# A two-layer hybrid trunk on one core: the mask product of the SSD rows left out, and new orders of work at four places

## The chip, the cores and the metric

The kernel runs on one core of a Trainium2 chip. The metric is the device time of one execution in microseconds. Of the kernel before there are three runs, 1043.61 to 1047.78, median 1046.85.

## The reference

One inference step of a decoder trunk with two layers, for 256 prompt tokens and 8 samples of 4 tokens, 288 columns that share all weights. The model width is 1024.

- Layer 0: norm, one input projection, then two head groups side by side: mLSTM (4 heads, key 128, value 256, with a gated state matrix) and SSD (16 heads of 64 in two groups that share B and C). Their outputs are joined for one output projection and added to the residual. A gated FFN with a causal convolution follows.
- Layer 1: norm, projection, retention (8 heads with rotary positions, value 256), output projection, residual and the same FFN. A last norm ends it.

What the change touches most is the SSD. For a head with running sums `acum` of its log decays it computes

```
seg   = acum[l] - acum[s]
decay = where(causal, exp(where(causal, seg, 0)), 0)
M     = (C B^T) * decay * dt
y     = M x + (C S) * exp(acum)
```

The log decays are negative, so `seg` is at most 0 wherever the mask holds. The states of all heads are outputs too.

## The kernel before, in words

**Weights and tiles.** Every matrix product has fp32 accuracy from three passes of fp32r: a weight chunk (128 x 1024, 512 KB, eight 128 x 128 blocks) is loaded to `raw`, ScalarE copies it to the high part `wh` (`split`, line 1222), VectorE subtracts to the low part `wl` (`split`, line 1627), and TensorE makes high x high, high x low and low x high (lines 806 to 808). All three buffers are rings of four chunks: SyncE's `stream` loads chunk c once the low part of chunk c-4 is made, ScalarE overwrites a slot once TensorE has read the chunk there. An output tile is 128 x 288 and takes eight blocks of K (24 matmuls), or more. The two mixer output projections have K = 16 blocks; their tiles go in groups of four, first halves first, so of the 16 chunks of the even one (numbered 0 to 15 here, from `E_OUT`) 0 to 3 are the first halves of tiles 0 to 3, 4 to 7 their second halves, 8 to 11 the first halves of tiles 4 to 7.

**Order.** Each engine has one program, an order written out by hand; semaphores join them. TensorE weaves head work between tiles. Its small products ("jobs", named `ass2.3`, `sbc5` and so on) and tiles use eight PSUM banks. `plan_banks` (lines 134 to 289) walks through TensorE's order and gives each job the next bank of a ring: "five" is banks 3 to 7, "mix" banks 4 to 7; tiles of the projections to the inside have banks 0 to 2, other tiles 0 to 3. Before a product TensorE waits until the former user of its bank is emptied (`claim`), by VectorE ("dve") or ScalarE ("act") as the plan says.

**mLSTM heads** (four tiles to a head). TensorE's `updates_a` (line 922, matmul 927) makes eight state updates from `kgm` and `vst`, the values in three stacked parts: ScalarE copies two of them (line 1467), GpSimd subtracts for the third (line 2315), VectorE adds the result to the state (line 1901). GpSimd's loop (lines 2304 to 2318) keeps convolution rows (`keep_x`), makes the low parts of a finished head (`back`, line 2210), fills the next convolution rows, builds masked queries and then writes `vst`. ScalarE's loop starts on line 1446. VectorE adds the sample output to `num` (line 1895) before the updates.

**SSD passes** (eight, two heads each; lines 1066, 1507, 1988). For each head `log_rows` (line 868) makes a row matrix 128 x 416 in PSUM with two matmuls: identity x `drop`, the mask (0 or -1e30), and a broadcast of the row of running sums (`sbc`). ScalarE's `decays` (line 1478) does three exponentials with the key's negative sum as bias and writes `E2`, four slots. VectorE multiplies by the group's scores `cbm` (line 2001), TensorE makes the outputs (`sy`, line 1026). The scores come through `cb0` and `cb1`, which ScalarE copies out (`masked_scores`, line 1472). A pass also turns x (`xn`), multiplies a tile of the projections (`filler`), and late passes take in and update the sample states (`si`, `sx`, `su`); GpSimd scales those states (line 2347), `xt` and `xws` (lines 2013, 1519, 2344) prepare them.

**SyncE in the SSD stage** (lines 751 to 773). It loads 11 states, then for each of 16 updated states waits for VectorE's update, stores the state and loads a later one. For the first five it calls `stream` for one more chunk of the even projection ahead of that wait.

**Retention heads** (eight, lines 1183 to 1203 on TensorE, 2116 to 2147 on VectorE). In head h the results of head h-1 are normalised and turned back, VectorE's `back` (line 1740) applies gain and gate, ScalarE and GpSimd make high and low parts. The last head is woven into the first halves of the odd output projection; its tile 3 has bank 3.

## Time and profile before

| | |
|---|---|
| median of three runs | 1046.85 us |
| profiled execution, its own time | 1046.8 us |
| span of the profile | 1045.0 us |
| mean granted TensorE clock | 0.98 |
| TensorE busy | 993.7 us (95%) |
| VectorE, ScalarE, GpSimd busy | 751.0, 559.9, 382.0 us |
| matmuls of line 806 (high x high) into a `hH` tile | 1160, mean 305 ns |
| low parts, line 1627 | 257, mean 1255 ns |
| high parts, line 1222 | 257, mean 1057 ns |

Times are from the start of the span. Matmuls are pipelined, so the duration of one is longer than the distance from one start to the next. A number in square brackets behind a row of a timeline is the engine's idle time before it, with the instruction that ended it. The stages: mLSTM heads to about 198, SSD passes to 264, even projection to 343, FFN, odd layer from 555, its output projection from 765, FFN to the end.

### The profile page before, as it was taken

The numbers are of one execution on the slowest core, as the hardware profiler recorded it, in microseconds if no ns is written. First come the engines' busy times: TensorE is split into PE (matmuls) and PEld (weight loads), VectorE is DVE, ScalarE is ACT, GpSimd is POOL, SyncE is SP. The second block draws the span as 40 slices with busy tenths as digits, with TensorE's granted clock in tenths as the row PEclk, the third lists the DMA queues.
The fourth block names the chain that finished last, engine by engine and source line by source line (L and its number), as shares of the span: only waits on it lengthen the run. The fifth ranks groups of instructions, "written<-read, shape, count | busy, mean of one in ns | idle before, by whom it ended". The sixth has DMA issues, their size and how long they took to land.

```text
span 1045.0 us, 19169 instructions
## 1 busy us (share of the span) xinstructions
PE 993.7 (95%) x7256; PEld 943.6 (90%) x7256; DVE 751.0 (72%) x1326; ACT 559.9 (54%) x932; POOL 382.0 (37%) x599
## 2 busy tenths in 40 slices
PE   7999998898779999999999999999979999999996
PEld 6999887777579999999999999899979999999996
DVE  5767688777856899996547857767755599899442
ACT  6535666633535666665444356656645565565431
POOL 4003214134201677774004531232221277777100
PEclk9989999999999999999999999999989999999999
DMA  8463364452455545455444745775634555445541
GB/s 300 136 230 122 109 205 147 133 172 92 141 208 187 171 169 162 163 167 191 162 167 157 262 141 172 221 232 191 201 135 147 176 168 175 162 164 169 188 142 46
DMA packets 64685, 177.22 MB, mean 170 GB/s; under 512 B 5889, under 2 KB 24065, under 8 KB 64593
## 3 DMA queue, kind: packets, MB, share of 16 engines
q1 hardware_dynamic: 64304, 174.86, 50.3%
q8 instruction: 58, 0.95, 0.4%
q0 software_dynamic: 288, 1.12, 0.3%
q14 instruction: 35, 0.28, 0.1%
HBM read 154.92 MB, written 21.05 MB: 168 GB/s over the span
## 4 chain that ended last, share of the span: by engine, by line
PE 85%; DVE 6%; ACT 3%; issue 3%; DMA 2%; POOL 1%; SPq 0%; DVEq 0%; ACTq 0%; POOLq 0%
PE bank L806 25%; PE bank L808 25%; PE bank L807 24%; PE bank L852 2%; DMA raw<-wts 2%; ACT wh L1222 1%; DVE wl L1627 1%; PE bank L1162 1%; PE bank L1130 1%; PE bank L1092 1%; PE bank L864 1%; POOL sts L2347 1%; DVE E L2001 1%; PE bank L859 0%; PE bank L1136 0%
## 5 line engine op out<-in xcount | busy, mean ns | idle before, releaser
L1222 ACT ACTIVATE wh<-raw 128x1024 fp32r<-128x1024 f32 x257 | 270.6, 1057 | 329.5 <-PE bank L808 317.7
L1627 DVE TENSOR_TENSOR wl<-raw,wh 128x1024 fp32r<-128x1024 f32 x257 | 321.8, 1255 | 167.9 <-ACT wh L1222 165.9
L806 PE MATMUL bank<-hH,wh 128*128 128x288 f32 x1160 | 353.9, 305 | 6.4 <-DVE wl L1627 4.1
L807 PE MATMUL bank<-hL,wh 128*128 128x288 f32 x1160 | 346.8, 299 | 0.0
L808 PE MATMUL bank<-hH,wl 128*128 128x288 f32 x1160 | 345.9, 298 | 0.0
L806 PEld LDWEIGHTS bank<-hH,wh 128*128 128x128 f32 x1160 | 222.2, 192 | 10.0 <-DVE wl L1627 3.2
L807 PEld LDWEIGHTS bank<-hL,wh 128*128 128x128 f32 x1160 | 222.3, 192 | 0.5
L808 PEld LDWEIGHTS bank<-hH,wl 128*128 128x128 f32 x1160 | 222.6, 192 | 0.0
L1750 DVE SCALAR_TENSOR_TENSOR cy<-pad,vec,cy 128x304 f32<-128x304 f32 (+1 forms) x212 | 140.7, 664 | 4.6 <-ACT cy L1270 0.6
L2188 POOL COPY pad<-fst 128x16 f32<-128x16 f32 x88 | 94.4, 1077 | 67.3 <-DVE cy L1750 67.3
L806 PE MATMUL bank<-upH,wh 128*128 128x288 f32 x352 | 104.4, 297 | 0.0
L808 PE MATMUL bank<-HH,wl 128*128 128x288 f32 x352 | 104.4, 296 | 0.0
L806 PE MATMUL bank<-HH,wh 128*128 128x288 f32 x352 | 104.0, 296 | 0.0
L807 PE MATMUL bank<-upL,wh 128*128 128x288 f32 x352 | 103.8, 295 | 0.0
L808 PE MATMUL bank<-upH,wl 128*128 128x288 f32 x352 | 103.5, 294 | 0.0
L807 PE MATMUL bank<-HL,wh 128*128 128x288 f32 x352 | 102.6, 292 | 0.0
L2168 POOL TENSOR_TENSOR hF<-hF 128x288 f32<-128x288 f32 x35 | 30.0, 856 | 190.7 <-ACT hF L1241 181.1
L1270 ACT ACTIVATE cy<-pad,vec 128x304 f32<-128x304 f32 (+1 forms) x100 | 63.1, 631 | 13.0 <-DVE pad L1664 8.8
L807 PEld LDWEIGHTS bank<-HL,wh 128*128 128x128 f32 x352 | 67.1, 191 | 0.0
L808 PEld LDWEIGHTS bank<-upH,wl 128*128 128x128 f32 x352 | 66.3, 188 | 0.0
L806 PEld LDWEIGHTS bank<-HH,wh 128*128 128x128 f32 x352 | 66.1, 188 | 0.0
L807 PEld LDWEIGHTS bank<-upL,wh 128*128 128x128 f32 x352 | 66.1, 188 | 0.1
(336 smaller groups left out, 1611.8 us busy)
## 6 DMA issues: line engine op xcount, KB each, us to landing
raw<-wts SPq DMA_DIRECT2D x257, 512.0 KB, 3.3
st<-r_in SPq DMA_DIRECT2D x9, 512.0 KB, 6.5
r_out<-st SPq DMA_DIRECT2D x9, 512.0 KB, 4.4
st<-c_in SPq DMA_DIRECT2D x8, 514.0 KB, 6.9
c_out<-st SPq DMA_DIRECT2D x8, 514.0 KB, 5.2
sts<-h_in SPq DMA_DIRECT2D x12, 256.0 KB, 6.1
h_out<-sts SPq DMA_DIRECT2D x12, 256.0 KB, 2.9
st3r<-r_in SPq DMA_DIRECT2D x4, 512.0 KB, 6.1
```

Source lines behind the costliest of these rows:

```text
L806: mm(out, h, xh, start=(k == 0), stop=False)
L807: mm(out, h, xl, start=False, stop=False)
L808: last = mm(out, lo, xh, start=False, stop=(k == K - 1))
L852: last = nc.tensor.transpose(out[0:n, g * P:(g + 1) * P], src[:, a:a + n], ident)
L864: mm(out[:, 0:TP], k[:, 0:P], q[:, 0:TP], start=True, stop=True)
L1092: last = mm(out[:, 0:T], ones, xbcT[:, 4 * g + i, :], start=(i == 0), stop=(i == 3))
L1222: s.do(act(wh[:, c % RING, :], raw[:, c % RING, :], ACT.Copy), hi_ready)
L1270: s.do(act(cy[:, n % 4, 0:width], x[:, 0:width], ACT.Identity, scale=tap, bias=bias), tap_done)
L1627: do(tt(wl[:, c % RING, :], raw[:, c % RING, :], wh[:, c % RING, :].bitcast(F32), ALU.subtract), lo_ready)
L1750: do(stt(out=y, in0=x[:, j:j + width], scalar=taps[j], in1=y, op0=ALU.mult, op1=ALU.add), conv_done if j == len(taps) - 1 else None)
L2168: do(tt(hF[:, 0, :], hF[:, 0, :], hF[:, i, :], ALU.add), ssq_ready if i == KD - 1 else None)
L2188: do(copy(padded(x, w)[:, :, 0:w], kept), fill_done)
```

## The change

Five places change.
1. SSD rows: the mask product of `sbc` is left out. VectorE's gate code now keeps the positive sum as the key's column; ScalarE makes max(0, column - row) with a ReLU, three activations a head, waits for its own last one, then two exponentials a head of the negative, for two heads together. Where the mask does not hold this is 1, so the mask moves to the scores: VectorE writes `cbm` as (drop >= -1) x score. VectorE waits for the new semaphore `decay_ready`.
2. mLSTM heads: ScalarE's two copies to `vst` stand at the start of the head, GpSimd's `vst` part ahead of `keep_x`, and its `back` behind the fills and queries.
3. SyncE: chunks of the even projection are streamed to 7 before the first stored state, to 9 before the fourth, to 11 before the ninth (exclusive ends).
4. Last retention head on TensorE and in the plan: head 6 is turned back before head 7's sample output, and its late jobs use the ring "mix".
5. Last retention head on VectorE: `back` of head 6 first, statistics ahead of the early updates.

The diff, cut to its core:

```diff
@@ constants, planner of banks @@
+MASKED = ((slice(0, P), slice(0, TP + P)), (slice(0, NS), slice(TP + P, BLK)))
...
-    for name in ("cb0", "bn0", "bn1", "sbc0", "sbc1"):
+    job("cb0", "dve", "five")
+    for name in ("bn0", "bn1", "sbc0", "sbc1"):
         job(name, "act", "five")
...
         if i == 0:
-            job("cb1", "act", "five")
+            job("cb1", "dve", "five")
...
         tile(group_tile(h, 3))
-        job(f"ros{h}", "dve", "five")
+        ring = "mix" if h == CH - 1 else "five"
+        if h == CH - 1:
+            turned_back("r", h - 1, ring)
+        job(f"ros{h}", "dve", ring)
         for b in EARLY_STATES:
-            job(f"rss{h}.{b}", "dve", "five")
-        if h:
+            job(f"rss{h}.{b}", "dve", ring)
+        if 0 < h < CH - 1:
             turned_back("r", h - 1, "five")
@@ SyncE @@
             for n in range(BG * NB):
                 g, b = divmod(n, NB)
-                if n < 5:
-                    stream(E_OUT + 4 + n)
+                if n in (0, 3, NB):
+                    stream(E_OUT + {0: 7, 3: 9, NB: 11}[n])
@@ TensorE @@
-            def log_rows(name, part, h):
+            def log_rows(name, part, h, masked):
...
-                mm(out[:, 0:BLK], identR[:], drop[:], start=True, stop=False)
-                mm(out[:, 0:BLK], one, rowS[part], start=False, stop=True).then_inc(mix_done, 1)
+                if masked:
+                    mm(out[:, 0:BLK], identR[:], drop[:], start=True, stop=False)
+                mm(out[:, 0:BLK], one, rowS[part], start=not masked, stop=True).then_inc(mix_done, 1)
...
             def sbc(h):
-                log_rows(f"sbc{h}", PARTS["ac"], h)
+                log_rows(f"sbc{h}", PARTS["ac"], h, False)
...
                 group(h, 3)
+                if h == CH - 1:
+                    back("r", h - 1, AH + h - 1)
                 sample_out(h)
                 updates(h, EARLY_STATES)
-                if h:
+                if 0 < h < CH - 1:
                     back("r", h - 1, AH + h - 1)
@@ ScalarE @@
                 step_a(t)
+                wait_empty(eng, f"v{2 * h + 1}")
+                if h:
+                    wait_job(eng, f"ass{h - 1}.{NB - 1}")
+                for row in ROW[0:2]:
+                    s.do(act(vst[row, 0:AV + 1], values_a(h, 2)[0:NS], ACT.Copy), vst_hi)
...
                 product(f"asp{h}", pout[:, h % 2, 0:AV + 1])
-                if h:
-                    wait_job(eng, f"ass{h - 1}.{NB - 1}")
-                for row in ROW[0:2]:
-                    s.do(act(vst[row, 0:AV + 1], values_a(h, 2)[0:NS], ACT.Copy), vst_hi)
...
-            def masked_scores(g):
...
-            def decays(h):
+            def gaps(h):
...
-                c = P + h
-                s.do(act(x[:, 0:TP], b[:, 0:TP], ACT.Exp, bias=cols[:, 0, c:c + 1]))
-                s.do(act(x[:, TP:TP + P], b[:, TP:TP + P], ACT.Exp, bias=cols[:, 1, c:c + 1]))
-                s.do(act(x[0:NS, TP + P:BLK], b[0:NS, TP + P:BLK], ACT.Exp, bias=cols[0:NS, 2, c:c + 1]), mix_act)
+                for g, n, a, z in ((0, P, 0, TP), (1, P, TP, TP + P), (2, NS, TP + P, BLK)):
+                    s.do(act(x[0:n, a:z], b[0:n, a:z], ACT.Relu, scale=-1.0, bias=cols[0:n, g, P + h:P + h + 1]),
+                         mix_act if g == 2 else None)
+
+            def decays(i):
+                for h in (2 * i, 2 * i + 1):
+                    gaps(h)
+                s.settle()
+                for h in (2 * i, 2 * i + 1):
+                    for part in MASKED:
+                        s.do(act(E2[:, h % 4, :][part], E2[:, h % 4, :][part], ACT.Exp, scale=-1.0),
+                             decay_ready if part[0].stop == NS else None)
...
-            masked_scores(0)
...
             decays(0)
-            decays(1)
             inverse(AH - 1)
...
                     back("a", AH - 1, y_even)
-                    eng.wait_ge(st_out[2], 32)
-                    masked_scores(1)
@@ VectorE @@
-                do(ts(slab[b16, 1, :], ac[b16, :], -1.0, None, ALU.mult))
+                do(copy(slab[b16, 1, :], ac[b16, :]))
...
             normalise("a", AH - 1, AH - 1)
+            def masked_scores(g):
+                wait_job(eng, f"cb{g}")
+                b = mb(f"cb{g}")
+                for part in MASKED:
+                    do(stt(out=cbm[g][part], in0=drop[part].bitcast(F32), scalar=-1.0, in1=b[part],
+                           op0=ALU.is_ge, op1=ALU.mult), mix_dve if part[0].stop == NS else None)
+                settle()
+            masked_scores(0)
...
-                        wait_empty(eng, f"sbc{h}")
-                        if h == HG:
-                            wait_empty(eng, "cb1")
+                        eng.wait_ge(decay_ready, h + 1)
...
                 if i + 3 < PAIRS:
                     xn(i + 3)
+                if i == 0:
+                    eng.wait_ge(st_out[2], 32)
+                    masked_scores(1)
...
             split(R_OUT + 3 + 3)
+            back("r", CH - 2)
             sample_out(CH - 1)
+            statistics("r", CH - 1, AH + CH - 1)
             updates(CH - 1, EARLY_STATES)
-            statistics("r", CH - 1, AH + CH - 1)
-            back("r", CH - 2)
             normalise("r", CH - 1, AH + CH - 1)
@@ GpSimd @@
             for h in range(AH):
+                eng.wait_ge(vst_hi, 2 * h + 2)
+                settle()
+                do(tt(vst[ROW[2], 0:AV + 1], values_a(h, 2)[0:NS], vst[ROW[0], 0:AV + 1].bitcast(F32), ALU.subtract), vst_ready)
+                settle()
                 keep_x(3 + 2 * h)
                 keep_x(4 + 2 * h)
-                if h > 1:
-                    back("a", h - 2, y_even)
                 if h + 1 < AH:
                     fill_x(6 + 2 * h)
                     fill_x(7 + 2 * h)
                     queries("a", h + 1, h + 1, qT[:, h + 1, :])
...
+                if h > 1:
+                    back("a", h - 2, y_even)
                 if h + 1 < AH:
                     split_keys("a", h + 1, h + 1)
```

## Rows read from the trace of the kernel before

**Rows 1.** Table by stage: us, busy of PE PEld DVE ACT POOL, PEclk, DMA, GB/s
```profile
215.00:260.00 45.00, 41.10 (x289) 32.09 (x289) 32.32 (x56) 17.92 (x43) 16.17 (x12) 1.00 0.39 130
...
290.00:312.00 22.00, 16.01 (x106) 14.99 (x105) 10.87 (x20) 8.12 (x13) 1.97 (x2) 0.94 0.61 211
...
560.00:600.00 40.00, 40.00 (x302) 40.00 (x302) 34.64 (x54) 12.75 (x12) 25.15 (x14) 1.00 0.71 237
...
765.00:790.00 25.00, 19.51 (x138) 18.80 (x137) 15.20 (x35) 11.03 (x19) 3.93 (x6) 0.86 0.31 100
```

**Rows 2.** TensorE's list of waits: who for whom, us in total, times, longest
```profile
PE bank L806 <- DVE wl L1627: 9.4, 4, 5.3
...
PE bank L927 <- ACT kgs L1311: 3.2, 2, 1.6
```

**Rows 3.** Timeline of TensorE, state updates of heads 2 and 3: start, us, what, idle before
```profile
161.65 0.72 PE L927 MATMUL bank<-vst,kgm 96*128 96x258 f32 x4 [2.32 <-issue]
...
184.60 0.73 PE L927 MATMUL bank<-vst,kgm 96*128 96x258 f32 x4 [2.58 <-issue]
...
188.89 1.47 PE L927 MATMUL bank<-vst,kgm 96*128 96x258 f32 x4 [0.36 <-DVE num L1895]
```

**Rows 4.** Timelines of VectorE and ScalarE, last mLSTM head
```profile
175.01 1.23 DVE L1627 TENSOR_TENSOR wl<-raw,wh 128x1024 fp32r<-128x1024 f32 x1 [2.33 <-ACT wh L1222]
...
181.98 0.84 ACT L1467 ACTIVATE vst<-vA 32x257 fp32r<-32x257 f32 x2
```

**Rows 5.** Timeline of TensorE, log products of one SSD head
```profile
213.49 0.46 PE L872 MATMUL bank<-drop,identR 128*128 128x416 f32 x1
...
213.88 0.46 PE L873 MATMUL bank<-rowS,foldR 64*128 64x416 f32 x1
```

**Rows 6.** ScalarE's timeline (two rows), then groups of lines 1288 and 1687
```profile
199.44 0.45 ACT L1484 ACTIVATE E<-bank,cols 128x256 f32<-128x256 f32 x1
...
201.00 0.28 ACT L1316 ACTIVATE sm<-sm,vec 128x3 f32<-128x3 f32 x1
...
L1288 ACT ACTIVATE E<-cst x8: 533/552/554, 608.0 to 737.0; 128x416 f32<-128x416 f32 x8
...
L1687 DVE SCALAR_TENSOR_TENSOR Sp<-bank,E 128x384 f32<-128x384 f32 x4 | 2.2, 550 | 0.0
```

**Rows 7.** Timelines of VectorE and TensorE ahead of the SSD passes
```profile
201.55 0.16 DVE L1721 TENSOR_TENSOR sm<-sm 128x3 f32<-128x3 f32 x1 [3.02 <-ACT sm L1318]
...
204.51 1.15 PE L852 MATMUL bank<-cst,xbcT 128*128 128x128 f32 x9
```

**Rows 8.** Timelines of TensorE and VectorE, SSD passes
```profile
219.79 0.44 PE L1032 MATMUL bank<-E,xdt 128*64 128x256 f32 x2 [1.03 <-DVE E L2001]
...
222.03 1.21 DVE L2001 TENSOR_TENSOR E<-E,cbm 128x384 f32<-128x384 f32 x4
...
244.30 3.76 DVE L2001 TENSOR_TENSOR E<-E,cbm 128x384 f32<-128x384 f32 x4
...
252.72 0.45 PE L872 MATMUL bank<-drop,identR 128*128 128x416 f32 x1 [1.96 <-DVE xbcT L2006]
```

**Rows 9.** Timelines of VectorE, SyncE and TensorE, even projection
```profile
259.56 1.23 DVE L1627 TENSOR_TENSOR wl<-raw,wh 128x1024 fp32r<-128x1024 f32 x1 [5.09 <-ACT wh L1222]
...
300.78 9.25 SPq L665 DMA_DIRECT2D raw<-wts  x5
...
309.82 0.58 PE L806 MATMUL bank<-vH,wh 128*128 128x288 f32 x1 [5.29 <-DVE wl L1627]
```

**Rows 10.** Timelines of VectorE and TensorE, odd projection
```profile
775.39 0.42 DVE L2101 TENSOR_TENSOR num<-bank,num 128x256 f32<-128x256 f32 x1
...
779.17 0.61 PE L806 MATMUL bank<-rvH,wh 128*128 128x288 f32 x1 [5.49 <-DVE yF L1740]
...
797.99 1.23 DVE L1627 TENSOR_TENSOR wl<-raw,wh 128x1024 fp32r<-128x1024 f32 x1 [1.28 <-ACT wh L1222]
...
801.53 1.23 DVE L1627 TENSOR_TENSOR wl<-raw,wh 128x1024 fp32r<-128x1024 f32 x1 [1.28 <-ACT wh L1222]
```

More of the change, by code:

```diff
@@ L1508, in _ @@
                 split(place(t + 2 + i, 0)[0] + 3)
-                for h in (2 * i + 2, 2 * i + 3):
-                    if h < BH:
-                        decays(h)
+                if i + 1 < PAIRS:
+                    decays(i + 1)
                 if i == 0:
                     back("a", AH - 1, y_even)
-                    eng.wait_ge(st_out[2], 32)
-                    masked_scores(1)
                 if i == 4:
@@ L1995, in _ @@
                     if h < BH:
[L1996 to L1998 removed]
+                        eng.wait_ge(decay_ready, h + 1)
                         x, c = E2[:, h % 4, :], cbm[h // HG]
[L2000 removed]
+                        for part in MASKED:
                             do(tt(x[part], x[part], c[part], ALU.mult),
```

12 lines of the change are left out of this document (2 added, 10 removed).

## The prediction

> **What bounds the kernel now.** I read the table by stage first, then TensorE's list of waits, then the timelines of the engines around each wait. By stage [rows 1] TensorE is nearly the whole time: in the SSD stage it works 41.10 of 45 us, in a plain stretch (560 to 600) all of 40 with 302 matmuls, 0.1325 us each. It idles 5.99 of 22 us at the end of the even projection (mean granted clock 0.94) and 5.49 of 25 around the odd one (0.86). The list of waits [rows 2] says that the largest is for the low weight part of VectorE (9.4 us, one of 5.3), and that two of 1.6 us in the mLSTM heads are for `kgs`, which ScalarE writes. So the edits can pay in two ways: less TensorE work, and waits that go. For each wait I ask what comes last once it is gone.
>
> **GpSimd's order in the mLSTM heads.** In head 2 and head 3 TensorE stands 2.32 and 2.58 us ahead of the state updates [rows 3]; GpSimd writes the low part of `vst` last there, behind the two `back` subtractions. Now ScalarE makes the copies at the start of the head and GpSimd subtracts at once, so this wait goes. In head 2 the fourth update still needs the bank that ScalarE empties after `kgs`, the 1.6 us wait of heads 0 and 1 [rows 2]: I book 0.4. In head 3 the next four updates already wait for VectorE's addition to `num` (0.36 at 188.89, the four stretched to 1.47) [rows 3]. TensorE comes 2.6 us earlier and waits for VectorE instead: zero. The price is that the copies (0.84) now precede the table loads and the next weight copy, for which VectorE waits 2.33 us [rows 4], and VectorE has no slack from there to the addition. `fill`, `queries` and `vst` leave the time in which VectorE normalises, which gives about that back. The bounds are a loss of 0.85 and a gain of 2.6. I take 0.5 us, nearer the loss, since VectorE's chain is what the rows show. The rows kept by GpSimd and its fills move by under 1 us; their reader, VectorE's convolution, is a tile later.
>
> **The mask product.** Each of 16 heads loses one 416-column product, 0.39 us from its start to the next (213.49 to 213.88) [rows 5]: 6.2 us of TensorE. Not all of it is on the path:
> heads 0 and 1 (0.8) lie ahead of a new wait. Bank 6 of `cb0` goes to `xn0`, and `cb0` is now emptied by VectorE, behind `normalise`, which waits 3.02 us for ScalarE's `inverse` [rows 7], behind the decays. ScalarE needs 1.56 us for six activations today (199.44 to 201.00) [rows 6]. The six ReLUs have the same sizes and a column as bias, so 1.56 again; then two exponentials for each head, from 0.55 for 416 columns [rows 6] about 0.6 a head with the small one, 1.3 a pair with the wait between. Today's `normalise` starts at 201.55; with 1.3 more, and 1.0 less for the earlier heads (0.5) and the score copy that ScalarE loses (0.5, an estimate from the same row), it starts about 201.8. Its three subtractions of 256 columns are each under the 0.55 us of a 384-column product [rows 6], 1.3 as an estimate, and the masked product is that 0.55 and a sample part, 0.8: 203.9. `xn0` starts at 204.51 now [rows 7]. TensorE would be there at 203 and waits for VectorE: only the earlier 0.5 stays.
> Heads 4 and 5 (0.8) lie ahead of 219.79, where TensorE waits 1.03 for VectorE's decay product [rows 8]. That comes late because GpSimd works beside it: such a group takes 3.76 us at 244.30 and 1.21 at 222.03 [rows 8]. GpSimd's work there neither shrinks nor moves. Heads 10 to 13 are eaten by the chain `xt`, `xws`, product (3.76), and head 14 by the wait of 1.96 at 252.72 [rows 8]. What counts is heads 2, 3, 6 to 9 and 15, seven times 0.39, 2.7; with 0.2 for products that find less of GpSimd beside them, 2.9. The bounds are 0, if every pass waits for VectorE, and 6.2.
> ScalarE's two exponentials more a pass cost nothing if the pass hides them. A pass is 6.3 us, first bias product to head products (213.49 to 219.79) [rows 5, 8], and about 5.5 afterwards; ScalarE then has 1.06 for the weight copy, 1.56 and 1.3, 3.9 in all. The decays are for the next pass, so they are wanted one pass later. If that cover failed, 1.3 us in each of eight passes, 10 us. The score copy that leaves ScalarE and the product that VectorE gains for group 1 lie beside TensorE's tile: zero, 0.8 if not. The change from a negation to a copy in the gates is one VectorE instruction for another: zero.
> The trace has no ReLU beside an exponential. The Trainium skill (ScalarE: Activation LUTs, "Table sets: the hidden batching unit") says that ReLU is in every table set, by which no load is added; no row here shows it.
> That ReLU is put on ScalarE is right by the rows: in the SSD stage it is busy 17.92 of 45 us and VectorE 32.32 [rows 1]. The Trainium skill's rule for this (ScalarE: Activation LUTs, "Rules for kernel authors") is the reverse, ReLU on VectorE; by it 1.5 us a pass would leave ScalarE for an engine on which TensorE already waits, and the mask's 2.9 would be about 0.
>
> **SyncE's order.** Today the weight chunks of the even projection are issued one for each stored state, so that chunk 4 arrives late (VectorE idle 5.09 us for it at 259.56) and chunk 8 is issued at 300.78, behind all stores; TensorE then waits 5.29 us at 309.82 [rows 9]. Now chunks 4 to 6 go ahead of the first store, 7 and 8 ahead of the fourth, 9 and 10 ahead of the ninth. Each asks only that the low part of the chunk four earlier is made, which VectorE does ahead of the updates for which the next store waits. Behind them in SyncE's queue are those stores and the loads of states 11 to 15; the wait for chunk 4's low part ends before the fourth update, so I book no delay. First place: VectorE no longer stands at 259.56. But TensorE was not waiting there, and the updates and products behind it run on: 0.7. Second place: 5.3 goes. Next in line is the loop of weight copy, low part, residual sum and square, which takes 3.54 us a chunk in the odd projection (797.99 to 801.53) [rows 10], against 3.2 for TensorE's 24 matmuls (24 x 0.1325 [rows 1]); for three chunks that gives 1.0 back. The stage's mean clock of 0.94 over 22 us [rows 1] is 2.6 us at 1.2 GHz, which costs 1.3; without the wait I book that too. Together 0.7 + 5.3 - 1.0 + 1.3 = 6.3. The bounds are 1, if the loop or a landing takes the wait's place, and 8.
>
> **The last retention head.** TensorE waits 5.49 us at 779.17 for bank 3, which VectorE empties in `back` of head 6, behind `sample_out`, two updates and the statistics [rows 10]. Now these jobs use banks 4 to 7, so the tile's bank is free, and VectorE does `back` first. `back` then runs where the sum stands now, at 775.39 [rows 10]. The second update takes the bank of the first turned half and waits for it till 775.9; with its products the tile starts at 776.3, 2.9 us earlier. TensorE stands about 2 us instead of 5.5. The stage's mean clock of 0.86 over 25 us [rows 1] is 7 us at 1.2 GHz; I give back 0.8 of the 3.5 that this costs. Sum 3.7. `normalise` of head 7 comes behind two updates instead of behind `back`, about as late, and TensorE asks for it a tile later. The bounds are 1.5 (the moved `back` waits for `normalise` of head 6 as well) and 6.5.
>
> **The sum.** 0.5 + 2.9 + 6.3 + 3.7 = 13.4 us. The profiled execution takes 1046.8 (span 1045.0, 1.8 around it), almost the median of 1046.85. 1046.8 - 13.4 = 1033.4.
>
> **The rivals.**
> *All waits go and nothing replaces them* (chance 0.12): heads 2.6, mask 6.2, SyncE 6.3 and odd projection 5.5, 20.6 us, 1026. For it speaks that each wait has one releaser; against it, VectorE's addition at 188.89 and GpSimd beside VectorE [rows 3, 8].
> *The chunks come early but another wait holds the even projection* (0.17): the loop, a landing or the last updates keep TensorE, and SyncE gives 1. With the rest that is 8.1 us, 1038.7. For it: the loop is slower than TensorE [rows 10]. Against it: both waits in those rows are for a chunk that was issued late [rows 9].
> *The new order does nothing measurable* (0.08): ScalarE's longer decays and `cb0` on VectorE's chain eat SyncE's gain, about 1045.
> *TensorE's clock falls in the SSD stage* (0.05), the slower end. Less work a pass and the same VectorE chain mean more idle in each pass. Idles of 1.03 and 1.96 us there leave the stage at 1.00 today [rows 1, 8], while the stretch with 5.49 is at 0.86 [rows 1]. If the idle of a pass grows to some 2 us, all eight passes run at 1.2 GHz: 24 matmuls take 3.2 us more, 26 in all, against a forecast of 1033.4: 1059. The Trainium skill tells of such a case (TensorE: Matmul & The Clock Gate, "A second HAM failure mode: psum-queue depth-cycling"): short idles between groups make the clock fall again and again. The rows of the SSD stage do not bear it out so far.
>
> **How the numbers follow.** My forecast has 0.58; its terms have most of their play in SyncE and the odd projection, 1030 to 1037. The range must reach the second rival and part of the first: 1027 to 1041. A difference under 0.5% (5.2 us) can't be told from none here; the three runs span 1043.6 to 1047.8. Faster by more: the forecast, the first rival and most of the second, 0.86. Same 0.09, slower 0.05.
>
> **What would show it.** Right: no wait over 1 us for the low part after the even updates; the last tile of the odd projection's first halves starts 2 to 3 us after the turned halves; `xn0` waits for `cbm`; the updates 4 to 7 of head 3 wait some 3 us for VectorE. Wrong: a table load between ReLU and exponential, a SyncE wait in front of a store that TensorE feels, or a lower clock in the SSD stage.

## The result, and the profile after

The changed kernel takes 1036.03 us (median of 6 runs, 1035.52 to 1038.05); the kernel before, beside it, 1044.45 (6 runs, 1042.25 to 1047.78). The ratio is 0.9914, with a 95% interval of 0.9892 to 0.9935: 9.0 us less, between 6.8 and 11.3. The forecast was 1033.4 in a range of 1027 to 1041, and 13.4 us less. The profiled execution takes 1036.3 (span 1034.5, mean granted clock 0.977; before 1046.8, 1045.0, 0.980).

In the new file the lines have moved: the matmuls of a tile are lines 812 to 814, the low part is 1634, the high part 1231, the state updates of the mLSTM heads 934, the row product of an SSD head 880, the E product 2017, sy 1039 to 1043.

The table by stage of the changed kernel (columns as in [rows 1]), the SSD passes in two pieces, then the even projection, a plain stretch and the odd projection:

```profile
213.00:241.00 28.00, 27.15 (x212) 22.24 (x211) 23.14 (x40) 19.70 (x54) 13.39 (x10) 1.00 0.53 180
241.00:256.00 15.00, 11.97 (x58) 9.00 (x58) 9.36 (x17) 5.66 (x16) 4.96 (x5) 0.66 0.41 141
...
300.00:315.00 15.00, 14.47 (x104) 13.65 (x103) 8.91 (x12) 9.85 (x15) 3.59 (x4) 1.00 0.63 200
560.00:600.00 40.00, 40.00 (x301) 40.00 (x301) 32.07 (x49) 12.74 (x12) 24.18 (x16) 1.00 0.71 237
755.00:780.00 25.00, 22.69 (x160) 21.59 (x160) 14.95 (x36) 12.42 (x20) 6.48 (x9) 0.93 0.44 146
```

The two projections have filled up (5.99 of 22 and 5.49 of 25 us of idle in [rows 1], now 0.53 of 15 and 2.31 of 25). The SSD stage, all at 1.00 before, has a piece at 0.66. TensorE's list of waits, as [rows 2]:

```profile
PE bank L812 <- DVE wl L1634: 6.2, 4, 3.3
PE bank L934 <- ACT kgs L1320: 4.2, 3, 1.6
PE bank L1039 <- DVE E L2017: 3.4, 2, 2.6
...
PE bank L858 <- DVE cbm L1957: 2.9, 1, 2.9
PE bank L934 <- DVE num L1902: 2.7, 1, 2.7
...
PE bank L1169 <- DVE yF L1747: 1.8, 1, 1.8
```

The wait of 5.3 (chunk 8) is gone and that of 5.49 (odd projection) has become 1.8; those for `cbm`, `num` and E are new or longer. Most of the 6.2 us that are left for low parts have nothing to do with the change: 3.32 and 2.13 stand at the start of the kernel, at 10.35 and 13.11 us (in the trace of the kernel before 1.37 and 2.13 at 8.94 and 11.70). The same in time, TensorE's timeline:

```profile
188.21 1.66 PE L934 MATMUL bank<-vst,kgm 96*128 96x258 f32 x4 [2.72 <-DVE num L1902]
...
204.36 1.18 PE L858 MATMUL bank<-cst,xbcT 128*128 128x128 f32 x9 [2.94 <-DVE cbm L1957]
...
231.08 0.65 PE L880 MATMUL bank<-rowS,foldR 64*128 64x416 f32 x2
231.66 0.55 PE L858 MATMUL bank<-cst,xbcT 128*128 128x128 f32 x3
...
244.15 1.12 PE L1039 MATMUL bank<-E,xdt 128*64 128x256 f32 x4 [2.64 <-DVE E L2017]
...
303.18 0.37 PE L812 MATMUL bank<-vH,wh 128*128 128x288 f32 x1 [0.17 <-DVE wl L1634]
...
769.04 0.68 PE L1169 MATMUL bank<-vst,kgm 96*128 96x256 f32 x2 [1.82 <-DVE yF L1747]
769.51 0.45 PE L812 MATMUL bank<-rvH,wh 128*128 128x288 f32 x1
```

Read against [rows 3, 7 to 10]: the updates 4 to 7 of the last mLSTM head wait 2.72 instead of 0.36; `xn0` stands 2.94 for the masked scores; two row products take 0.58 to the next instruction; sy5 stands 2.64 and is then made at half the clock (1.12 for four, 0.65 elsewhere); chunk 8 stands 0.17. From chunk 7 to chunk 8 it was 8.75 us (301.07 to 309.82) and is 3.63 (299.55 to 303.18).

VectorE around the two new waits:

```profile
202.41 0.16 DVE L1728 TENSOR_TENSOR sm<-sm 128x3 f32<-128x3 f32 x1 [4.89 <-ACT sm L1327]
...
203.58 0.63 DVE L1957 SCALAR_TENSOR_TENSOR cbm<-drop,bank 128x384 f32<-128x384 f32 x2
...
228.30 0.46 DVE L1662 TENSOR_TENSOR zT<-bank,rstd 128x288 f32<-128x288 f32 x1 [0.81 <-PE bank L814]
...
238.98 1.34 DVE L1634 TENSOR_TENSOR wl<-raw,wh 128x1024 fp32r<-128x1024 f32 x1 [2.08 <-ACT wh L1231]
240.25 3.75 DVE L2017 TENSOR_TENSOR E<-E,cbm 128x384 f32<-128x384 f32 x4
```

And ScalarE:

```profile
199.10 1.64 ACT L1488 ACTIVATE E<-bank,cols 128x256 f32<-128x256 f32 x6
...
200.78 1.18 ACT L1497 ACTIVATE E<-E 128x384 f32<-128x384 f32 x4
...
235.73 2.14 ACT L1526 ACTIVATE xws<-xt 32x1024 fp32r<-32x1024 f32 x2 [1.28 <-DVE xt L2032]
237.89 1.06 ACT L1231 ACTIVATE wh<-raw 128x1024 fp32r<-128x1024 f32 x1
```

Six ReLUs and four exponentials of a pair take 1.64 and 1.18 (forecast 1.56 and 1.3), with no table load between. Ahead of sy5 the order of reading is: ScalarE waits 1.28 us for VectorE's `xt`, copies `xws` (2.14) and then the weights, VectorE stands 2.08 us for that weight copy, and the E product that TensorE wants is behind it on VectorE. The same chain stands in the kernel before, VectorE's rows first, then TensorE's:

```profile
232.38 0.46 DVE L1655 TENSOR_TENSOR zT<-bank,rstd 128x288 f32<-128x288 f32 x1 [1.78 <-PE bank L808]
...
243.06 1.32 DVE L1627 TENSOR_TENSOR wl<-raw,wh 128x1024 fp32r<-128x1024 f32 x1 [2.08 <-ACT wh L1222]
...
248.21 0.65 PE L1032 MATMUL bank<-E,xdt 128*64 128x256 f32 x4 [0.92 <-DVE E L2001]
```

From the emptying of a filler tile (`zT`) to the end of that E product VectorE takes 15.7 us in both (232.38 to 248.06 before, with the E product of [rows 8], 228.30 to 244.00 now). TensorE has four mask products less to make in that time, and so it waits 2.64 us instead of 0.92.

At xn0 TensorE is 0.15 us ahead of the kernel before (204.36 against 204.51), at xn7 5.0 (231.66 against 236.69), and at chunk 7 only 1.5 (299.55 against 301.07).

### The profile page after: what moved, and what is told of

Same layout as the page of the kernel before. It is cut to its first block, busy times and chain, and to the rows that moved or that the text cites. A ratio compares the mean times of both kernels' runs of the same rounds, so it can differ in the third digit from the quotient of the medians.

```text
span 1034.5 us, 19173 instructions
## 1 busy us (share of the span) xinstructions
PE 990.0 (96%) x7240; PEld 939.6 (91%) x7240; DVE 746.4 (72%) x1330; ACT 567.5 (55%) x960; POOL 380.0 (37%) x599
## 3 DMA queue, kind: packets, MB, share of 16 engines
q0 software_dynamic: 288, 1.12, 0.3%
## 4 chain that ended last, share of the span: by engine, by line
PE 85%; DVE 7%; ACT 4%; issue 3%; DMA 1%; POOL 0%; DVEq 0%; SPq 0%; ACTq 0%; POOLq 0%
PE bank L812 25%; PE bank L814 24%; PE bank L813 24%; PE bank L858 2%; ACT wh L1231 2%; DVE wl L1634 1%; PE bank L1169 1%; PE bank L1137 1%; DVE E L2017 1%; PE bank L1099 1%; PE bank L870 1%; DMA raw<-wts 1%; PE bank L1143 0%; DVE hL L2061 0%; PE bank L865 0%
```

## The experiments

Twelve kernels, each beside runs of the kernel before on the same chip. Ratios are to it. A trace shows one execution, which can lie some microseconds from the median of its kernel.

| kernel | median us (runs) | before | ratio, 95% interval |
|---|---|---|---|
| SyncE alone | 1037.62 (12) | 1043.66 | 0.995, 0.9929 to 0.9971 |
| last retention head alone | 1041.47 (12) | 1043.66 | 0.9979, 0.9956 to 1.0003 |
| no mask product alone | 1040.56 (12) | 1043.66 | 0.9971, 0.9955 to 0.9987 |
| vst order alone | 1044.95 (12) | 1043.66 | 1.0015, 0.9993 to 1.0038 |
| changed, E first | 1029.19 (4) | 1042.88 | 0.986, 0.9839 to 0.988 |
| changed, inverse first | 1034.51 (6) | 1042.88 | 0.9912, 0.9893 to 0.9932 |
| changed, sy5's wait filled | 1035.24 (6) | 1042.88 | 0.9925, 0.9909 to 0.9941 |
| changed, E and inverse first | 1028.49 (4) | 1042.88 | 0.986, 0.9841 to 0.9879 |
| + sy emptied first | 1023.76 (6) | 1044.21 | 0.9796, 0.9763 to 0.9829 |
| + silus early | 1020.38 (6) | 1044.21 | 0.977, 0.9735 to 0.9806 |
| sy first + filled heads | 1018.27 (6) | 1044.21 | 0.9743, 0.971 to 0.9777 |
| all, with fillings | 1016.68 (5) | 1043.44 | 0.975, 0.9718 to 0.9781 |

### The parts, each alone on the kernel before

**SyncE alone.**

```diff
-                if n < 5:
-                    stream(E_OUT + 4 + n)
+                if n in (0, 3, NB):
+                    stream(E_OUT + {0: 7, 3: 9, NB: 11}[n])
```

> The kernel before with SyncE's three stream calls alone. Theory (each part has its own place): the even output projection's tiles of 5.29, 1.3 and so on stop waiting for wl, the stage after it starts 5 to 6 us earlier, time -5.0 to -6.5 us (ratio 0.9938 to 0.9952); profile: first tile of chunk 8 ends its claim with a wait under 0.5 us, and norm L849 or its counterpart comes 5 to 6.5 us earlier. Rival A (the chunks only looked late: without the SSD stage's own 1.5 us the same wait moves to another chunk): -1 to -2 us. Rival B (the earlier weight reads collide with the SSD state reads): si1 and the sn0 stretch come later by over 1 us and the time moves by less than 4 us.

Measured: 5.2 us less (3.0 to 7.4). TensorE at chunk 8:

```profile
300.48 0.38 PE L806 MATMUL bank<-vH,wh 128*128 128x288 f32 x1 [0.17 <-DVE wl L1627]
```

The wait is 0.17 instead of 5.29, and the next three chunks wait 0.11 each. The theory holds; rivals A and B don't. The norm behind the projection comes 9.7 us earlier than in the trace of the kernel before (333.5 against 343.2), more than the 5 to 6.5 expected; but 4.2 of that stood already at chunk 7 (296.85 against 301.07), most of it from ahead of the SSD passes, where the two programs are the same.

**The last retention head alone** (the changes to plan, TensorE and VectorE named as 4 and 5).

```diff
                 group(h, 3)
+                if h == CH - 1:
+                    back("r", h - 1, AH + h - 1)
                 sample_out(h)
...
+            back("r", CH - 2)
             sample_out(CH - 1)
+            statistics("r", CH - 1, AH + CH - 1)
             updates(CH - 1, EARLY_STATES)
-            statistics("r", CH - 1, AH + CH - 1)
-            back("r", CH - 2)
```

> The kernel before with the reordered last retention head alone (plan, TensorE and VectorE). Theory: the wait of 5.49 for yF in the odd output projection becomes about 1.8, all else as before, time -3.3 to -3.8 us (ratio 0.9964 to 0.9968). Rival (in the changed kernel the head gained only since the stage before it ended in another clock state or with other weights in hand): less than -2 us, and the wait for yF stays over 3.

Measured: 2.2 us less, with an interval from 0.3 more to 4.6 less; 3.3 to 3.8 were expected. TensorE there:

```profile
778.85 0.80 PE L1165 MATMUL bank<-vst,kgm 96*128 96x256 f32 x2 [1.83 <-DVE yF L1745]
779.45 0.44 PE L809 MATMUL bank<-rvH,wh 128*128 128x288 f32 x1
```

The wait is 1.83 as in the changed kernel, so the rival falls. From the start of the two tiles of group 3 to the rest of the projection it takes 18.53 us (767.88 to 786.41), against 20.82 before (764.99 to 785.81) and 17.24 in the changed kernel (758.07 to 775.31): 2.3 and 3.6 less. The tile behind the wait took 5.89 us here, 4.73 there and 5.58 before; how much of it falls in a stretch at 1.2 GHz is the difference. This trace is of the longest of the twelve runs (1047.96 us).

**The SSD rows without the mask product, alone.**

```diff
-                mm(out[:, 0:BLK], identR[:], drop[:], start=True, stop=False)
-                mm(out[:, 0:BLK], one, rowS[part], start=False, stop=True).then_inc(mix_done, 1)
+                if masked:
+                    mm(out[:, 0:BLK], identR[:], drop[:], start=True, stop=False)
+                mm(out[:, 0:BLK], one, rowS[part], start=not masked, stop=True).then_inc(mix_done, 1)
...
+                    s.do(act(x[0:n, a:z], b[0:n, a:z], ACT.Relu, scale=-1.0, bias=cols[0:n, g, P + h:P + h + 1]),
+                         mix_act if g == 2 else None)
```

> The kernel before with the SSD rows without the mask product alone (row matmuls, relu and exp on ScalarE, masked scores on VectorE, the slab copied unnegated). Theory: a pair of row jobs takes 0.57 to 0.59 on TensorE instead of 1.54, xn7 comes 4 to 5 us earlier, but the late xws weights and E product and the half clock behind it give most of it back, and the even projection still waits for the weights that SyncE issues late: 0 to -1.5 us at the end (ratio 0.9985 to 1.000), with the wait for wl of chunk 8 longer than 5.29. Rival A (the mask product is worth its full time): -3 to -5 us (ratio 0.995 to 0.997). Rival B (the new wait at xn0 and the slower stage behind it cost more than the products save): +0.5 to +3 us.

Measured: 3.0 us less (1.4 to 4.7), twice the most that I expected after seeing the changed trace, and the lower end of what rival A gives. By stage and at chunk 8:

```profile
228.00:240.00 12.00, 10.57 (x79) 8.94 (x75) 9.74 (x14) 9.70 (x24) 9.28 (x7) 1.00 0.00 1
240.00:253.00 13.00, 10.96 (x49) 8.55 (x49) 7.43 (x14) 3.51 (x11) 3.10 (x3) 0.61 0.44 136
```

```profile
302.57 0.58 PE L809 MATMUL bank<-vH,wh 128*128 128x288 f32 x1 [4.93 <-DVE wl L1628]
```

The stretch at 0.61 behind sy5 stands here and in none of the other three, so it comes with this part; over the twelve runs the mean granted clock is 0.976, against 0.980 over the 35 of the kernel before. Rival A's reason falls with that: the products alone are 6.2 us, and the interval ends at 4.7. What I had wrong is the wait for chunk 8: it did not grow, it is 4.93. SyncE issues that chunk behind stores that wait for VectorE's updates, and these came earlier too (the issue is at 293.89 instead of 300.78), so the late chunk moved along and swallowed nothing.

**The vst order alone** (ScalarE's part is shown; the same lines go further down, and GpSimd's order is that of the change).

```diff
                 step_a(t)
+                wait_empty(eng, f"v{2 * h + 1}")
+                if h:
+                    wait_job(eng, f"ass{h - 1}.{NB - 1}")
+                for row in ROW[0:2]:
+                    s.do(act(vst[row, 0:AV + 1], values_a(h, 2)[0:NS], ACT.Copy), vst_hi)
```

> The kernel before with the earlier vst copies and difference alone (ScalarE and GpSimd in the mLSTM heads). Theory: the waits of 2.32 and 2.58 before the updates of heads 2 and 3 are replaced, in head 2 by kgs (about 1.0 to 1.3) and in head 3 by num (about 2.7 in the next four updates), so sbc0 comes within 0.8 us of where it was: 0 to -0.8 us (ratio 0.9992 to 1.000). Rival A (waits removed and not replaced): -1.5 to -2.6 us. Rival B (ScalarE's copies ahead of the gates delay products and keys): +0.5 to +1.5 us.

Measured: 1.6 us more by the ratio, with an interval from 0.7 less to 4.0 more. TensorE in heads 2 and 3:

```profile
157.92 0.39 PE L927 MATMUL bank<-vst,kgm 96*128 96x258 f32 x1 [0.33 <-DVE Sp L1690]
159.31 0.39 PE L927 MATMUL bank<-vst,kgm 96*128 96x258 f32 x1 [1.01 <-ACT kgs L1311]
...
186.50 1.66 PE L927 MATMUL bank<-vst,kgm 96*128 96x258 f32 x4 [2.71 <-DVE num L1896]
```

The waits are replaced as expected: 2.32 by 0.33 and 1.01, 2.58 by 2.71. From the kgs product of head 1 to the first row products it takes 60.0 us (135.48 to 195.49), against 60.2 (137.96 to 198.16). Nothing in this trace costs 1.6 us, but it is of one of the shorter runs (1040.73, the median is 1044.95), and the interval holds zero; whether this part helps or harms by a microsecond or two stays open.

The four ratios multiply to 0.9915, the whole change is 0.9914: as far as intervals of some 2 us on each can tell, the parts do not fight each other.

### What the mask product's time was given back to

Beside the times, the traces of the kernels that follow can be compared from the first row product to the norm behind the even projection, a stretch that leaves out what differs from run to run ahead of it:

| trace | from, to | us |
|---|---|---|
| changed | 197.15, 336.23 | 139.1 |
| E first | 194.00, 330.04 | 136.0 |
| inverse first | 193.62, 329.76 | 136.1 |
| sy5's wait filled | 195.28, 334.41 | 139.1 |
| E and inverse first | 193.91, 326.68 | 132.8 |
| + sy emptied first | 195.94, 321.45 | 125.5 |
| + silus early | 193.89, 319.08 | 125.2 |
| sy first + filled heads | 191.50, 316.10 | 124.6 |
| all, with fillings | 191.16, 315.76 | 124.6 |

**E first** on the changed kernel.

```diff
-                    split(place(t, 0)[0] + 3)
                 for h in (2 * i, 2 * i + 1):
...
                             do(tt(x[part], x[part], c[part], ALU.mult),
                                e_ready if part[0].stop == NS else None)
+                if i < PAIRS:
+                    split(place(t, 0)[0] + 3)
```

> The changed kernel, but in every pass of the SSD stage VectorE multiplies E by the masked scores before it makes the pass's wl, instead of after. Theory (the 2.64 before sy5 and the 0.77 before sy1 are VectorE held at wl, which waits for a wh that stands behind the xws copies on ScalarE, and the 10.2 us at 1.2 GHz follow the idle): both waits fall under 0.3, no stretch at 1.2 GHz between 240 and 255, sy6 from 254.68 to 247 or 249, time -3 to -6 us against the changed kernel (1030 to 1033). Rival A (the E product is slow beside GpSimd, 3.75 us, and is late wherever it stands): the wait before sy5 stays over 1.5 and the time moves less than 1 us. Rival B (later wl makes the tiles wait): new waits for wl of over 1 us in passes 1 to 7, time 0 to +3.

Measured: 0.986, 5.6 us below the 0.9914 of the changed kernel (0.0054 of 1043; the two were measured beside different runs of the kernel before, and the intervals don't touch); the traces give 3.0 of it. The waits before sy1 and sy5 are gone. Another has come up, on TensorE:

```profile
242.46 0.71 PE L880 MATMUL bank<-rowS,foldR 64*128 64x416 f32 x1 [2.73 <-DVE xbcT L2023]
```

On VectorE:

```profile
231.82 4.05 DVE L2016 TENSOR_TENSOR E<-E,cbm 128x384 f32<-128x384 f32 x4
...
238.10 2.74 DVE L2016 TENSOR_TENSOR E<-E,cbm 128x384 f32<-128x384 f32 x4
...
241.91 0.50 DVE L2023 SCALAR_TENSOR_TENSOR xbcT<-xbcT,vec,bank 128x288 f32<-128x288 f32 x1
```

The second row job of the last pair needs sy5's bank, and VectorE empties that behind the next E product and the low part. It is the wait of 1.96 of [rows 8], which grew, and the clock falls behind it. So the cause of the wait at sy5 is the theory's, VectorE held at the low part ahead of E, and my expectation that no stretch at 1.2 GHz would be left was wrong.

**The inverse first**, on ScalarE.

```diff
+            inverse(AH - 1)
             decays(0)
-            inverse(AH - 1)
```

> The changed kernel, but ScalarE makes the inverse of the last mLSTM head before the first pair of decays instead of after. Theory (the 2.94 before xn0 is VectorE waiting for sm, which stands behind the relus and exps): VectorE's idle time of 4.89 falls to about 2, the wait before xn0 to under 0.5, sy0 comes 2 to 2.9 us earlier; at the end -1 to -3 us against the changed kernel, as later waits grow by part of it. Rival (the pair of decays, 0.5 us later, or the bn copies hold the stage): the wait before xn0 moves to sy0 and the end moves less than 0.7 us.

TensorE there:

```profile
198.50 0.74 PE L858 MATMUL bank<-cst,xbcT 128*128 128x128 f32 x5 [0.62 <-DVE cbm L1957]
...
238.31 0.65 PE L1039 MATMUL bank<-E,xdt 128*64 128x256 f32 x4 [2.63 <-DVE E L2017]
...
242.82 0.71 PE L880 MATMUL bank<-rowS,foldR 64*128 64x416 f32 x1 [1.77 <-DVE xbcT L2022]
```

The wait of xn0 went from 2.94 to 0.62; sy5 still waits 2.63, and the row job's wait went from 0.39 to 1.77. The ratio, 0.9912, is that of the changed kernel; on top of E first it also moves nothing that the times can tell (0.986 twice). The trace does not show where the gain went. In it nothing is lost: the stretch in the table is 2.9 us shorter. But it is of the shortest run, 1029.70 us with a mean clock of 0.982, and the other five took 1034.25 to 1036.10 with 0.976 and 0.977. Whether the inverse's place is worth nothing or 3 us stays open.

**sy5's wait filled** with six products that sy5 overwrites, E as late as before.

```diff
                 out = free_bank(f"sy{i}")
+                for _ in range(6 if i == 5 else 0):
+                    mm(out[:, 0:BLK], identR[:], drop[:], start=True, stop=True)
```

> The changed kernel, and six products of identity and mask (into sy5's own bank, overwritten by sy5) on TensorE in the place of the idle time before sy5; nothing else moves, so E stays late. Theory (the clock falls because TensorE stands idle there): TensorE is at 2.4 GHz through sy5, su and the next tile, which take 0.65, 0.95 and 3.45 instead of 1.12, 1.65 and 5.45; sy6 comes 2.5 to 4 us earlier, time -2 to -4.5 us against the changed kernel. Rival (the clock falls there for what went before, or for another reason, or the fall only moves to the next wait): the stretch at 1.2 GHz between 243 and 254 stays, or comes within 10 us, time -0.5 to +1.5 us.

```profile
239.53 1.29 PE L1036 MATMUL bank<-drop,identR 128*128 128x416 f32 x6
242.23 0.65 PE L1041 MATMUL bank<-E,xdt 128*64 128x256 f32 x4 [1.41 <-DVE E L2019]
...
246.83 0.71 PE L880 MATMUL bank<-rowS,foldR 64*128 64x416 f32 x1 [2.22 <-DVE xbcT L2024]
```

On TensorE's timeline the six take 1.29 us, so 1.41 of the 2.64 stays idle. sy5 runs at 2.4 GHz (0.65). That the filling did this is not shown, since in the trace of the inverse first sy5 takes 0.65 too, behind 2.63 us without any filling. And the time saved is handed on: the row job waits 2.22, and the next tile is at 1.2 GHz all the same. The ratio of 0.9925 and the table (139.1, as in the changed kernel) show no gain. Up to the row job VectorE sets the pace here and not the clock, and behind it the clock falls as it did. The theory's price was wrong, and its cause stays open at this place.

**Both first**, E and the inverse.

> Both reorderings, E before wl on VectorE and the inverse before the decays on ScalarE. Theory: the two gains add for the most part, -4 to -8 us against the changed kernel (1028 to 1032), and the even projection's weights do not become late again (waits for wl under 1 us from chunk 7 on). Rival (SyncE's second place is at its limit): the wait for wl comes back at chunk 8 with 1 to 4 us, and both together give no more than the better one alone.

Measured: 0.986. The wait for weights stays at 0.17 at chunk 8, so that rival falls, but "no more than the better one alone" is what the times say; the trace, of the shortest of four runs, gives 3.3 us more than E first.

**sy emptied first**, on top of both: VectorE's addition of sy of the pass before stands ahead of E.

```diff
+                if i:
+                    m = i - 1
+                    wait_job(eng, f"sy{m}")
+                    do(stt(out=xbcT[:, m, :], in0=xbcT[:, m, :], scalar=v("D", m), in1=mb(f"sy{m}")[:, 0:T],
+                           op0=ALU.mult, op1=ALU.add), mix_dve)
                 for h in (2 * i, 2 * i + 1):
```

> Both reorderings of before (E ahead of wl on VectorE, the inverse ahead of the decays on ScalarE), and VectorE empties sy of the pass before ahead of E too. Theory (the 2.73 before the second row job of the last pair is its bank, held by sy5, which VectorE empties only behind a 2.73 E product and a 1.21 wl): that wait falls under 0.5, the next tile stays at 2.4 GHz, sn0 comes 2 to 4 us earlier, time -1 to -4 us against both reorderings alone (1025 to 1028). Rival (E is then late in its turn, behind sy's product): waits before sy1 to sy6 of 0.5 to 1.5 each come up, and the time moves by less than 1 us.

Measured: 0.9796, 6.7 us below the 0.986 of both, more than the 4 that I expected at most; the traces say 7.3. By stage, heads and passes:

```profile
100.00:191.00 91.00, 83.45 (x586) 73.60 (x586) 72.29 (x160) 60.69 (x121) 24.52 (x41) 0.95 0.48 153
...
200.00:265.00 65.00, 61.97 (x435) 47.91 (x433) 54.14 (x103) 42.33 (x107) 29.42 (x21) 0.97 0.52 179
```

No wait of passes 1 to 7 is left, and what is at 1.2 GHz lies at sn0, which still waits 2.43 for ScalarE. With the three reorderings the SSD stage gives 0.9914 - 0.9796 = 0.0118, some 12 us, more than the whole change did.

**Silus early**, on top of sy first. On VectorE the products of the first four gates stand ahead of scaling `xdt`; on ScalarE:

```diff
             for i in range(PAIRS):
+                if i == PAIRS - 1:
+                    for j in range(8):
+                        wait_tile_empty(eng, T0 + FILL + j)
+                        s.do(act(zT[:, j, :], zT[:, j, :], ACT.Silu), zs_ready)
+                    log_and_exp()
                 split(place(t + 2 + i, 0)[0] + 3)
```

> The same as the one before it, and the eight silus of the gates with their two table loads stand on ScalarE after the last decays instead of after the last wh, and VectorE multiplies the first four gates ahead of scaling xdt. Theory (the 2.42 before sn0 is the chain wh, table load, silus, table load, gate products, squares): the wait falls under 0.6, no stretch at 1.2 GHz at sn0, time -2 to -4 us against the one before it. Rival (the silus push the wh of chunks ahead and the wait for wl comes back, or sx1 and sn1 take up what sn0 gives): less than 1 us.

Measured: 0.977, 3.4 us less in the medians; the intervals overlap. The wait before sn0 went from 2.43 to 1.32, not under 0.6, but the clock holds. The passes and sn0 by stage:

```profile
200.00:265.00 65.00, 61.99 (x435) 47.85 (x434) 52.74 (x102) 42.71 (x106) 31.03 (x23) 1.00 0.50 171
```

A gain is not shown: in the traces the stretch in the table is 0.3 us shorter (125.2 and 125.5). Behind sn0 TensorE now waits 1.1 us for a state update and 0.55 for a state's load, so what sn0 gives is taken up, as the rival said, though not at the places that it named.

### What the idle time in the heads costs

**Filled heads**, on top of sy first (without the early silus).

```diff
                     out = free_bank(f"ass{h}.{b}")
+                    for _ in range((6, 6, 4, 0)[h] if b == 2 else 0):
+                        mm(out[:, 0:BLK], identR[:], drop[:], start=True, stop=True)
```

Twelve more of them stand ahead of the last tile of head 3, in its bank.

> As the first of this call, and products of identity and mask on TensorE in the mLSTM heads: 6, 6 and 4 in the bank of the third update of heads 0 to 2 ahead of the 1.59, 1.55 and 0.99 waits, 12 in the bank of the last tile of head 3 ahead of the 2.72 wait; they are overwritten. Theory (the clock falls behind these waits since TensorE stands idle): the stretches at 1.2 GHz at 135, 159 and 186 us vanish, the tile behind each takes 3.4 instead of 4.9, time -2 to -5 us against the first. Rival A (the falls move to other waits nearby): the sum of the stretches from 100 to 200 us stays at 10.2 us and the time within 1 us. Rival B (the products hold up the updates and the chain behind them): +1 to +3 us.

Measured: 0.9743, 5.5 us under sy first in the medians. The intervals of the ratios overlap by 0.0014, but the runs themselves do not: 1016.19 to 1020.37 with the products, 1021.53 to 1025.19 without. By stage:

```profile
100.00:191.00 91.00, 87.31 (x627) 77.46 (x625) 74.92 (x168) 63.02 (x123) 23.53 (x36) 1.00 0.48 153
```

The same 91 us ran at 0.95 without the products. All eight traces with this order of the heads and without the products have three stretches at 1.2 GHz there, the two with them have none. Here TensorE itself sets the pace behind the waits, and 28 products whose results nobody reads make the kernel faster. One stretch came up at the first row jobs, 193 us, behind a wait of 2.03.

**All together**: the early silus, the filled heads, and two more places.

```diff
-                turn(f"bn{g}", xbcT[:, 8 + g, :])
+                turn(f"bn{g}", xbcT[:, 8 + g, :], 7 * g)
...
                     out = free_bank(f"rss{h}.{b}")
+                    for _ in range(10 if (h, b) == (CH - 1, EARLY_STATES[0]) else 0):
+                        mm(out[:, 0:CV], kgm[STACK, b, :], vst[STACK, 0:CV], start=True, stop=True)
```

> All reorderings so far (E and sy ahead of wl, the inverse and the silus earlier) with the products in the mLSTM heads, seven more ahead of the turn of bn1 (before the wait of about 2.0 at the first row jobs) and ten repeats of the first update's product in the last retention head (before the wait of about 1.8 for yF). Theory (each wait filled keeps 2.4 GHz behind it, and the early silus give their 2 to 3 us with it as without): no stretch at 1.2 GHz between 100 us and the end's last 8 us, 1012 to 1016 us. Rival A (the stretches that are left move on, one or two stay): 1016 to 1018.5. Rival B (the ten repeats or the seven products hold up what comes after them): 1019 or more.

```profile
100.00:1000.00 900.00, 889.43 (x6636) 846.82 (x6635) 670.35 (x1187) 514.27 (x866) 362.07 (x554) 1.00 0.52 173
```

TensorE is at 2.4 GHz from 100 to 1000 us in this execution. That is the theory's trace, and its time, 1015.17, is in the theory's range; but the median, 1016.68, falls in rival A's. The mean clock of the five runs goes from 0.992 to 0.997 (0.996 in the trace), so in some of them stretches at 1.2 GHz were left. The ratio, 0.975, can't be told from the 0.9743 of filled heads, and the table says the same (124.6 twice). Both beat the changed kernel's 0.9914 by some 1.7%.

## Why the prediction was right, point by point

**SyncE (6.3).** Right in mechanism, 5.2 alone (3.0 to 7.4). The second place gave 8.75 - 3.63 = 5.1 where 5.3 stood. The loop came as priced at 1.0: four chunks of the changed kernel start 3.54 us apart (303.18, 306.72, 310.26, 313.80), three times 0.36 more than the 3.18 of 24 matmuls, though only 0.13, 0.11 and 0.12 of that shows as idle time. From chunk 8 to the norm it takes 33.05 us (303.18 to 336.23) instead of 33.34 (309.82 to 343.16), as 1.3 back from the clock and 1.0 for the loop say. In the first place VectorE does not stop standing: it stands 5.53 us at 255.94, since ScalarE's copy there now waits for TensorE. What TensorE gained by it can be read only in SyncE's part alone, 0.9 us from xn0 to sn0 (64.83 against 65.76), where 0.7 was booked.

**The last retention head (3.7).** The wait of 5.49 became 1.82, as forecast ("about 2 us instead of 5.5"), and the two traces give 3.6 and 2.3. The times say 2.2 and can't tell it from 3.7, nor from nothing. That the rest of the wait lets the clock fall again was in the sum (0.8 of 3.5 given back). In the changed kernel it gave back more (0.93 over 25 us, 1.75 lost), in this part's own trace nothing (0.86 as before, 5.89 for the tile, 5.58 before): how much of the tile falls in the slow stretch differs from run to run. The tile starts 3.3 us after the turned halves, a little behind the 2 to 3 that were given as a sign.

**The heads (0.5).** The waits were replaced by `kgs` (booked 0.4, measured 1.01, with 0.33 for `Sp` ahead of it) and by `num` (foretold as about 3, measured 2.72). The term is not told from zero.

**The mask product (2.9).** The size came out, 3.0 alone, but by two errors that cancel, which is luck. The first: a row product leaves 0.48 a head, not 0.39. Two heads took 1.53 (235.16 to 236.69 before) and take 0.58 (231.08 to 231.66), since the one that stays also starts closer behind its neighbour (0.29 instead of 0.39). That is 7.6 us in 16 heads, and 4.9 of it had arrived between xn0 and xn7. The second is the step that failed: the price of what is eaten. "Heads 10 to 13 are eaten by the chain `xt`, `xws`, product" came as said, but the sum books zero for it, and eaten time is idle time on TensorE. The wait before sy5 grew from 0.92 to 2.64, and behind it TensorE was at 1.2 GHz for some 10 us: the next tile took 5.45 us instead of 3.45, and from sy5 to sy6 it is 10.53 (244.15 to 254.68) instead of 8.66 (248.21 to 256.87). That this follows the longer wait and not something else in that part is argued, not shown: with the inverse first the same wait of 2.63 is followed by a sy5 at 2.4 GHz, and the fall comes some 2 us later (sy5 to sy6 10.05). The cover of ScalarE's longer passes did hold there: ScalarE had finished its exponentials and stood 1.28 us for `xt` ahead of the copies, and VectorE's stand of 2.08 for the weight copy is the same before and after. E first, which takes the low part and its wait out of VectorE's chain, brings 5.6 us by the times and 3.0 by the traces.

**The wait of xn0 for `cbm`** came, 204.36 against the 203.9 forecast for the masked scores.

**The rivals.** "The clock falls in the SSD stage" came in part: one piece at 0.66, not all eight passes, so it cost a few microseconds (1.9 from sy5 to sy6) and not 26. The Trainium skill's case (TensorE: Matmul & The Clock Gate, "A second HAM failure mode: psum-queue depth-cycling") is borne out by these traces in kind: waits of 1 to 3 us between groups of products were followed by 1.2 GHz in the heads and at or behind sy5, though not each of them, and filling those of the heads brought 2.4 back. "Another wait holds the even projection" did not come: nothing over 0.17 from chunk 8 on. "All waits go" did not come either; those for `num`, `cbm` and `yF` are in the list above.

**The sum** was 13.4 and the runs show 9.0 (6.8 to 11.3), so it was too high: by the parts alone SyncE 1.1 and the retention head 1.5, the mask right, and the heads 0.5 expected where the ratio shows a loss of 1.6. Each of these is within the interval of its part; only the whole is told. The time came closer than the saving, 1033.4 against 1036.03, and that is luck too: the sum starts from the profiled 1046.8, and six runs of the kernel before have a median of 1044.45. A start 2.4 too high took off half of a saving 4.4 too large.

## What to carry to other kernels

When work is taken off the bounding engine, go through the next engine's whole order in that stage, pass by pass, with everything that happens once in it: the pass with an extra copy is where the saving stops. Time that is eaten there is not zero: add it to the wait that stands there already, and ask what the clock does behind a wait of that length. On an engine that runs in order, what the bound waits for (E, an emptied bank) should stand ahead of what is wanted three chunks later. Then look at the granted clock by stage: a wait that can't be removed may still be worth filling, but only where TensorE and not another engine sets the pace behind it.

## What was not expected of the hardware

**Most of the spread of this kernel's runs goes with the clock.** Over 35 runs of the kernel before, spans go from 1036.0 to 1049.5 us and mean clocks from 0.970 to 0.988, with a correlation of -0.85. A profile of one run, compared with one of another, has that in it.

**Short idle times bring 1.2 GHz, but not each of them.** With E and the inverse first the tile behind the wait of 1.55 in head 1 takes 4.88 us, and so does the one behind 0.99 in head 2; with the heads filled the waits are 0.42 and 0.36 and the tiles 3.36 and 3.35. In the first of these traces the wait of 1.59 in head 0 had no such sequel (3.35), in the kernel before one of 1.60 at the same place had it (4.87), and the one of 2.58 [rows 3] had none. At sy5 too the traces differ: 1.12 behind a wait of 2.64 in the changed kernel, 0.65 behind 2.63 with the inverse first, where the clock falls some 2 us later.

**The E product takes 1.21 us or up to 4.05** for the same four instructions, by what GpSimd does beside it (3.75 at 240.25, where GpSimd scales states from 239.32 for 5.64 us). The Trainium skill (SBUF — State Buffer, "Who interferes with whom") says that a VectorE instruction with two inputs in SBUF contends with a GpSimd one that reads SBUF, and that one with a single SBUF input, outside VectorE's modes that use both ports, does not. The traces agree: the low part, also with two, took 1.94 at 245.10, beside GpSimd's last scaling (244.92), instead of 1.23, the addition of sy at 243.93, with one input in PSUM, 0.49 as always. No run takes GpSimd's work away from there, so the cause is read from what stands side by side.

**Two row products without the identity between them** start 0.29 us apart, not 0.39, so a product taken out can save more than its own distance.
